# A two-layer decoder kernel: first squares moved from GpSimd to ScalarE, x loaded beside h, a written-out order for the first 24 product steps, gate products spread through hq1

## The reference, cut to what matters

```python
def trunk_layer(h, ...):
    xn = rms_norm(h, norm_pre_mix)          # h * rsqrt(mean(h*h) + eps) * w
    proj = xn @ w_in
    hq, hf, hi, hg, aq, ak, av, gq, gk, gv, g_lr, gr = jnp.split(proj, split_points, axis=-1)
    f = lb_h + (1.0 - lb_h) * jax.nn.sigmoid(heads(hf, HG_HEADS))
    ...
    log_a = jax.nn.log_sigmoid(g_lr @ gla_w_gate2 + gla_b_gate) / GLA_TAU
    o_g, s_gla_new = gated_linear_recurrence(gq * GLA_DK ** -0.5, gk, gv, log_a, s_gla)
```

## Time and profile before

| | |
|---|---|
| three runs | 1828.49, 1833.54, 1835.95 us; median 1833.54 us |
| the profiled execution's own time | 1833.51 us |
| its span (first to last instruction) | 1831.7 us |
| busy: PE, DVE, ACT, POOL | 1722.6, 845.8, 635.8, 100.8 us: 94%, 46%, 35%, 6% of the span |
| mean granted TensorE clock | 0.975 of full speed |

### The profile page before, as it was taken

The page is one execution under the profiler, slowest core; times in us unless marked ns, Lnnn a source line. Parts: engine busy times, 40 slices in busy tenths (PEclk is TensorE's granted clock), DMA queues, the critical chain, the costliest instruction groups (busy, mean ns, idle before and its releaser), DMA issues.

```text
span 1831.7 us, 35825 instructions
## 1 busy us (share of the span) xinstructions
PE 1722.6 (94%) x16090; PEld 1604.4 (88%) x16090; DVE 845.8 (46%) x1304; ACT 635.8 (35%) x934; POOL 100.8 (6%) x110
## 2 busy tenths in 40 slices
PE   5999888999999999999999998888999999999998
PEld 5888775588999999999988887755989999999988
DVE  5423776636423333335745147754354143333364
ACT  3323324645323222233443323255453231222332
POOL 3002301000000000000000131100000000000000
PEclk9999898999999999999999999989999999999999
DMA  6521509942745726362363124299319366355311
GB/s 252 188 63 57 185 2 364 377 181 70 280 156 196 240 82 221 103 205 81 113 222 104 62 69 156 90 377 345 122 63 349 100 221 222 115 185 183 122 64 64
DMA packets 61081, 304.55 MB, mean 166 GB/s; under 512 B 7169, under 2 KB 8833, under 8 KB 59265
## 3 DMA queue, kind: packets, MB, share of 16 engines
q1 hardware_dynamic: 53504, 201.80, 30.9%
q0 software_dynamic: 7424, 100.47, 16.0%
HBM read 291.62 MB, written 111.08 MB: 220 GB/s over the span
## 4 chain that ended last, share of the span: by engine, by line
PE 83%; DVE 9%; ACT 3%; issue 2%; DMA 2%; SPq 0%; POOL 0%; DVEq 0%; ACTq 0%
PE pair L1844 15%; PE pair L1846 15%; PE pair L1845 15%; PE pair L866 2%; PE pair L848 2%; PE pair L849 2%; PE pair L850 2%; PE pair L868 2%; PE pair L1155 2%; PE pair L870 2%; PE pair L1924 2%; PE pair L1023 2%; PE pair L794 1%; PE pair L1911 1%; PE pair L796 1%
## 5 line engine op out<-in xcount | busy, mean ns | idle before, releaser
L1844 PE MATMUL pair<-x_hi_part,w_hi_part 128*128 128x288 f32 x1088 | 322.2, 296 | 2.1 <-DVE tmp L2230 2.1
L1845 PE MATMUL pair<-x_lo_part,w_hi_part 128*128 128x288 f32 x1088 | 321.0, 295 | 0.0
L1846 PE MATMUL pair<-x_hi_part,w_lo_part 128*128 128x288 f32 x1088 | 319.9, 294 | 0.0
L2167 DVE TENSOR_TENSOR w_lo_part<-raw,w_hi_part 128x1024 fp32r<-128x1024 f32 x154 | 188.8, 1226 | 235.2 <-ACT w_hi_part L2011 235.1
L1844 PE MATMUL pair<-u_hi_part,w_hi_part 128*128 128x288 f32 x928 | 274.7, 296 | 0.0
L1845 PE MATMUL pair<-u_lo_part,w_hi_part 128*128 128x288 f32 x928 | 273.8, 295 | 0.0
L1846 PE MATMUL pair<-u_hi_part,w_lo_part 128*128 128x288 f32 x928 | 272.8, 294 | 0.0
L2011 ACT ACTIVATE w_hi_part<-raw 128x1024 fp32r<-128x1024 f32 x154 | 161.8, 1051 | 210.3 <-PE pair L1846 208.3
L1844 PEld LDWEIGHTS pair<-x_hi_part,w_hi_part 128*128 128x128 f32 x1088 | 203.8, 187 | 2.5 <-DVE tmp L2230 2.5
L1846 PEld LDWEIGHTS pair<-x_hi_part,w_lo_part 128*128 128x128 f32 x1088 | 204.9, 188 | 0.0
L1845 PEld LDWEIGHTS pair<-x_lo_part,w_hi_part 128*128 128x128 f32 x1088 | 204.3, 188 | 0.0
(11 more groups left out here) (295 smaller groups left out, 3440.9 us busy)
## 6 DMA issues: line engine op xcount, KB each, us to landing
raw<-w_units SPq DMA_DIRECT2D x210, 512.0 KB, 3.6
ck_out<-ck POOLq DMA_DIRECT2D x16, 3060.0 KB, 14.6
arena<-cv SPq DMA_DIRECT2D x24, 640.0 KB, 8.4
arena<-ck SPq DMA_DIRECT2D x18, 640.0 KB, 10.5
more<-ck SPq DMA_DIRECT2D x18, 640.0 KB, 13.4
tail<-cv SPq DMA_DIRECT2D x18, 640.0 KB, 9.6
h<-ck SPq DMA_DIRECT2D x12, 640.0 KB, 12.8
y_out<-h SPq DMA_DIRECT2D x16, 288.0 KB, 2.1
```

Source lines behind the costliest of these rows:

```text
L1844: nc.tensor.matmul(out, wh[:, cols], xh[:, k, t], start=n == 0, stop=False)
L1845: nc.tensor.matmul(out, wh[:, cols], xl[:, k, t], start=False, stop=False)
L1846: mm = nc.tensor.matmul(out, wl[:, cols], xh[:, k, t], start=False, stop=n == KT - 1)
L2167: return tt_(dst, src, hi.bitcast(F32), ALU.subtract).then_inc(*up(done, 1))
```

## The change

1. **Squares.** POOL's eight squares go. ACT squares (`square_first`): tiles 0 and 1 after it has done the leading parts of tiles 0 to 5; then unit 2, the leading parts of tiles 6 and 7, and the squares of tiles 2 to 7, then unit 3. DVE follows the same order and no longer waits for a square before a remainder.
2. **Loads.** x goes to a place of its own (X_FIRST, in the arena) instead of h; SP waits for par before it issues tiles 2-3; unit 2 goes ahead of tiles 6-7.
3. **Order of the first 24 steps.** `FIRST_STEPS` writes it out for each layer; `sum_pre` comes after 19 steps in layer 0 and after 12 in layer 1.
4. **Gate products.** The four matmuls of z0 and z1 go between the steps of hq1 (after its k = 1, 2, 3, 4) and into pairs 2 and 3.
5. **gq0's evac** and the split of unit 9 go between the second and the third scan.
6. **Units 0 and 1 of layer 1** are split behind gate5 and gate6 instead of gate6 and gate7.

Nothing in the diff adds or removes a product, and no warming product is in either kernel.

```diff
+FIRST_STEPS = [[(0, 0), (0, 1), (0, 2), (0, 3), (1, 0), (0, 4), (1, 1), (0, 5), (2, 0), (1, 2), (0, 6), (2, 1), (1, 3),
+                (2, 2), (1, 4), (2, 3), (1, 5), (2, 4), (1, 6), (2, 5), (0, 7), (1, 7), (2, 6), (2, 7)],
+               [(u, k) for u in range(2) for k in range(6)] + [(u, k) for u in range(2) for k in (6, 7)]
+               + [(2, k) for k in range(KT)]]
+SUM_AT = [19, 12]
-            return pair[3 if name == "sum_pre" else 2 if name in APART else Q[name] % 2]
+            return pair[3 if name in ("sum_pre", "z1") else 2 if name in APART or name == "z0" else Q[name] % 2]
...
+        X_FIRST = arena[:, 4608:4608 + KT * T].rearrange("p (k t) -> p k t", k=KT)
+        SQ_FIRST = tail[:, 5248:5248 + KT * T].rearrange("p (k t) -> p k t", k=KT)
...
             first_unit(0)
             pair_of_tiles(0)
+            sp.wait_ge(s_par0, 16)
             pair_of_tiles(1)
             first_unit(1)
             pair_of_tiles(2)
-            pair_of_tiles(3)
             first_unit(2)
+            pair_of_tiles(3)
...
-        @block.gpsimd
-        def _(pool):
-            for k in range(KT):
-                if k % 2 == 0:
-                    pool.wait_ge(s_x[k // 2], 16)
-                nc.gpsimd.tensor_tensor(SQ_FIRST[:, k], H[:, k], H[:, k], ALU.mult).then_inc(*up(sq_pre, 1))
+        def square_first(k):
+            nc.scalar.activation(SQ_FIRST[:, k], X_FIRST[:, k], ACT.Square).then_inc(*up(sq_pre, 1))
...
+            for k in range(6):                       # ACT, ahead of the layers
                 if k % 2 == 0:
                     act.wait_ge(s_x[k // 2], 16)
-                next_hi(act, k)
+                next_hi(act, k, X_FIRST)
                 if k == 3:
                     first_hi(act, 1, 0)
+            for k in range(2):
+                square_first(k)
...
-            for k in range(KT):                      # DVE, ahead of the layers
-                dve.wait_ge(sq_pre, k + 1)
-                next_lo(dve, k, 0)
+            for k in range(6):
+                next_lo(dve, k, 0, X_FIRST)
                 if k == 3:
                     first_lo(dve, 1, 0)
-                if k >= 1:
-                    add_square(dve, k, 0, lambda j: SQ_FIRST[:, j])
+            add_square(dve, 1, 0, lambda j: SQ_FIRST[:, j])
...
-                for s in range(KT + BEHIND[-1]):
-                    if s == KT - 2:
+                for n, (u, k) in enumerate(FIRST_STEPS[layer]):
+                    if n == SUM_AT[layer]:
                         sum_pre()
...
+                        if name == "hq1" and 1 <= k <= 4:
+                            z, half = divmod(k - 1, 2)
+                            mz = nc.tensor.matmul(home(f"z{z}")[:, half, 0:HALF], ...)
...
+                    act.wait_ge(s_x[3], 16)          # ACT, layer 0, between units 2 and 3
+                    next_hi(act, 6, X_FIRST)
+                    next_hi(act, 7, X_FIRST)
+                    for k in range(2, KT):
+                        square_first(k)
...
+                if layer == 0:                       # DVE, between units 2 and 3
+                    next_lo(dve, 6, 0, X_FIRST)
+                    next_lo(dve, 7, 0, X_FIRST)
+                    for k in range(2, KT):
+                        add_square(dve, k, 0, lambda j: SQ_FIRST[:, j])
...
                 for r in range(4):
+                    if r == 2:
+                        evac("gq0", 32.0 ** -0.5)
+                        split_w(9)
                     nc.vector.tensor_tensor_scan(B[:, r], RESET, LV[0][:, r], 0.0, ALU.mult, ALU.add).then_inc(*up(b_ready, 1))
-                evac("gq0", 32.0 ** -0.5)
-                split_w(9)
...
-                    if k >= KT - FIRST and layer + 1 < DEPTH:
-                        first_hi(act, k - KT + FIRST, layer + 1)
+                    if 5 <= k < 5 + FIRST and layer + 1 < DEPTH:
+                        first_hi(act, k - 5, layer + 1)
```

More of the change, by code:

```diff
@@ L797, in steps @@
                     return mm
-                for s in range(KT + BEHIND[-1]):
-                    if s == KT - 2:
+                begun = set()
+                for n, (u, k) in enumerate(FIRST_STEPS[layer]):
+                    if n == SUM_AT[layer]:
                         sum_pre()
[L802 to L807, removed]
+                    if u not in begun:
+                        begun.add(u)
+                        if layer > 0:
+                            pe.wait_ge(*at(lin_ev, u - 1))
+                        if u < FIRST:
                             pe.wait_ge(w0_split, FIRST * layer + u + 1)
-                        elif s == lag:
+                        else:
                             pe.wait_ge(*at(w_split, u - FIRST + 1))
-                        if 0 <= s - lag < KT:
-                            mm = steps(home(IN1[u]), w_hi_part(u), w_lo_part(u), s - lag)
-                            if s - lag == KT - 1:
-                                mm.then_inc(*up(lin_mm, 1))
+                    pe.wait_ge(xn_split, KT * layer + k + 1)
+                    mm = steps(home(IN1[u]), w_hi_part(u), w_lo_part(u), k)
+                    if k == KT - 1:
+                        mm.then_inc(*up(lin_mm, 1))
                 for i, name in enumerate(IN1):
@@ L823, in _ @@
                         mm = steps(ps, wh, wl, k)
-                    mm.then_inc(*up(lin_mm, 1))
-                    if name == "hq0":
-                        pe.wait_ge(*at(s_par0, 0))
-                        pe.wait_ge(*at(lin_ev, Q["gq1"] + 1))
-                        for z in range(2):
-                            ps = claim(f"z{z}")
-                            for half in range(2):
-                                mm = nc.tensor.matmul(ps[:, half, 0:HALF], par[64:80, W_G2 + P * z:W_G2 + P * (z + 1)],
-                                                      Q4[64:80, 3, half * HALF:(half + 1) * HALF], start=True, stop=True)
-                            mm.then_inc(*up(lin_mm, 1))
+                        if name == "hq1" and 1 <= k <= 4:
+                            z, half = divmod(k - 1, 2)
+                            mz = nc.tensor.matmul(home(f"z{z}")[:, half, 0:HALF], par[64:80, W_G2 + P * z:W_G2 + P * (z + 1)],
+                                                  Q4[64:80, 3, half * HALF:(half + 1) * HALF], start=True, stop=True)
+                            if half == 1:
+                                mz.then_inc(*up(lin_mm, 1))
+                    mm.then_inc(*up(lin_mm, 1))
                 for g in range(2):
```

58 lines of the change are left out of this document (30 added, 28 removed).

## The result

| | before | after |
|---|---|---|
| median of the runs made side by side | 1836.58 us (6 runs, 1828.49 to 1842.82) | 1819.42 us (6 runs, 1817.72 to 1821.93) |
| the profiled execution's own time | 1833.51 us | 1821.93 us |
| its span | 1831.7 us | 1820.1 us |
| busy PE, DVE, ACT, POOL | and the table above | 1724.5, 839.0, 640.0, 91.5 us |
| mean granted clock | 0.975 | 0.975 |

The changed kernel takes 0.9915 of the time of the one before (95% interval 0.9893 to 0.9937), 1819.42 us against a forecast of 1812.5 and a range that ended at 1819. More runs of the kernel before moved its median up: 1836.58, not the 1833.54 of the three runs shown.

The account below looks back on a forecast made before the run. TensorE, on 83% of the chain, was taken as the bound, with savings only where PE idles or runs at low clock. 9.5 + 0.85 + 2.2 + 5.2 + 0.85 + 2.4 = 21.0 off 1833.5 gave 1812.5 us, range 1807 to 1819.

Parts of the forecast that it names:

- part 3: gq0's evac, both layers: gk1 starts earlier, PE then stands 1.8 us ahead of vs0; saves 2.2 and 2.4 us.
- should shift as a whole: Everything after the changed places waits on semaphores, not times, so it moves earlier unchanged; forecast difference 0.
- part 2: z0 and z1 strewn in hq1, both layers: the clock holds, 10.15 us becomes 9.3; saves 0.85 each.
- part 1: Layer 0 up to the end of hq0: earlier PE start, no starving, new 1.75 us wait at hq0; saves 9.5 us.
- the table product: Rival, chance 0.18: POOL's product of the tables (L717) precedes DVE's remainder in layer 0, PE idles 4.7 us at hq0; 1817.
- the clock falls in more places: Rival, chance 0.08: half clock also at z and at the stalls of 1.75 and 1.8 us; all five places give 1820.
- Part 4: Start of layer 1: earlier splits and new order remove 3.6 us of idle and 1.6 of clock; saves 5.2 us.
- slower: Rival, chance 0.03: shifted short waits newly tip into half clock, 1.6 us each; with 24 of them 1851 us.

Follow-up runs that it names:

- a1: Changed kernel with only gq0's evac between the second and third scan, unit 9's split behind gk0's evac: 1813.93 us, 0.9871 of the kernel before.
- a3: Changed kernel with the squares back on POOL: 1828.19 us, 0.9950 of the kernel before.
- b1: Changed kernel with units 0 and 1 of layer 1 split late again, behind gate6 and gate7, new order kept: 1823.95 us in one run.
- b2: Changed kernel with layer 1's first 24 steps in the old order, early splits of units 0 and 1 kept: 1824.32 us in one run.
- a4: Changed kernel with the four gate matmuls in one block behind k = 1 of hq1, both layers: 1828.89 us in one run.
- c0: The changed kernel again, unedited: 1816.73 us, 0.9895 of the kernel before.
- b3: Changed kernel without SP's wait for par between the first two pairs of tiles of x: 1814.26 us in one run.
- d3: Changed kernel with POOL's cache copy released earlier, so its product of the tables gets in ahead of DVE: 1821.37 us in one run.
- b4: Changed kernel with a1's edit, layer 0's sum of squares after 14 steps instead of 19, and gate products in two pairs: 1812.17 us, 0.9869 of before.

## Why the forecast missed

Two terms failed that the sum put at nothing: the clock behind the new stall at vs0 (part 3), and everything behind vs0 ("should shift as a whole"). The gate products were mis-sized (part 2), and the base was 2.8 us too low. The waits that the change removes and makes were foreseen rightly, and a1, a3, b1 and b2 show their causes. That the parts add up to 20.2 for 21.0 is in part luck: 0.55 too much saved in part 1 stands against 1.1 too little in part 2.

**Part 1 (9.5, measured 10.05)** was right in its steps. PE started 0.7 us sooner than 9.6, the wait ahead of hq0 was 1.55 for 1.75, no step starved between. The slow matmuls at the start lasted 5.9 us for the 5.65 taken; over all eleven profiles of changed kernels it is 2.9 to 6.0 us, up to 1.5 us of time from one execution to the next. a3 shows the mechanism: the place of the squares is worth 6.65 us up to the sum, and in a3 the table product came ahead with it.

**Part 2 (0.85 in each layer, measured 0.28)** was right that the clock holds (a4), and wrong in the size. I had taken 0.53 for a product and 0.2 for a change of kind. A single one holds PE for 0.68 (42.77 to 43.45) and costs another 0.19 on both sides, 0.87 in all (9.87 less 6.4, over four), where 0.73 was reckoned. The price of 0.53 is that of a product in a row of its own kind. So the term of the gate products, 2.9 us a layer with the changes of kind, should have been 3.5.

**Part 3 (2.2 and 2.4, measured 2.08 and 2.32)** was right in the idle, 1.75 for 1.8, and in its cause (a1). The step that failed stands between the lines of it: a stall of 1.8 us ahead of vs0 was taken to leave the clock high, because one of 1.91 had the earlier trace rows. Both were followed by half clock in the first profile, 1.7 us each, one in layer 0, one in layer 1. In other profiles with the same idle the clock held in both layers (c0, b3, d3), fell in layer 1 alone (b1, b2, a3) or in both (a4): 7 of 16 places in all, 5 of 8 in layer 1. The idle of 1.56 at hq0 kept it in each of seven profiles. This is the rival *the clock falls in more places*, which had a chance of 0.08, for two of its five places. The ranking behind it (1.91 leaves the clock, 2.40 lowers it) was one row for each side, and the kernel before already contradicted it. PE stands 2.42 us ahead of 867.32 and the clock stays:

```profile
867.32 0.40 PE L1956 MATMUL pair<-x_hi_part,w_hi_extra 128*128 128x288 f32 x1 [2.42 <-DVE x_lo_part L2167]
```

```profile
862.00:885.00 23.00, 17.31 (x121) 16.04 (x121) 19.30 (x46) 9.51 (x19) 0.00 (x0) 1.00 0.19 65
```

In the same trace an idle of 1.89 us ahead of 304.54 (L1074) was followed by half clock from 306.5. The length of an idle alone does not tell.

**Part 4 (5.2)** was right to the tenth; b1 and b2 show that of its two causes the order counts for most, 4.8 us without the splits, against 1.6 for the splits without the order. (Before the wait PE did two full steps, not less than two, as 12 matmuls from 922.14 to 923.61 show; the sum does not use it.)

**"What follows should shift as a whole"** is the other step that failed. The same instructions, from vs0 to layer 1's start and from vs0 to the end, took 837.5 and 837.7 us in the one profile of before, and 839.3 and 841.9 on average in the eleven profiles with a changed front (835.8 to 848.1). c0 shows that this need not come with the edit: its two stretches took 837.07 and 838.29. In layer 1 the average is one of two groups, and what parts them is whether the clock fell at vs0 (the table under c0). So the two failed steps are not apart: the stall was worth more than its own stretch where the clock fell. In the 22 runs of before that have a clock listed, the time falls by about 1 us for each 0.001 of mean granted clock (1830.24 at 0.977, 1838.48 at 0.968). The rival *slower* had named the mechanism, stretches that newly tip, with the price of 1.6 each. I gave it only the case of 19 or more, and left the case of six out of the range. Six is what the first profile has: 92.2 us of half clock where the 88.7 of before, less the five stretches that went, leave 71.6. At 1.6 each that is 9.6, against the 8.6 measured.

**The base.** The sum was made against 1833.5 us, and the median over more runs of the kernel before is 1836.05 to 1836.58. By 1836.3, in place of 1833.5, the forecast would have been 2.8 higher, and with the parts as measured (20.2 for 21.0) 0.8 higher again: 1816.1. The two medians measured are 1819.42 and 1816.73. So of the 6.9 us by which the first is over the forecast, 3.6 are the base and the size of the parts, above all of z, and 3.3 are what is left for the stretches behind vs0 (0.6 by the second). How much of this is chance, and how much a lasting effect of where the stalls now fall, these runs leave open: two medians of one kernel 2.7 us apart, with ranges that overlap, do not tell it.

## What to carry to other kernels

When a piece of work is moved ahead of a stall, move that piece alone: a second one that rode along (the split of unit 9) waited for another engine and made a new stall of nearly 2 us, and undoing it was worth as much as the move. Follow each new stall through to the end before pricing it, and give a stall near 2 us half the price of a half-clock stretch on top (7 of 16 here), with a longer range towards slow: where the clock fell at vs0 of layer 1, the rest of the kernel was 7.8 us longer on average. Do not take one row as proof that an idle of that length is harmless. Matmuls of another kind are cheapest in pairs between full steps: single ones pay the change each time, four in a row cost the clock.

## What was not expected of the hardware

- One idle of 1.75 us was followed by half clock in one execution and by full clock in the next, in the same kernel; one of 1.48 with the sum's tiny products behind it was followed by it in b4, and one of 2.42 at 867.32 in the kernel before was not.
- The first matmuls ran at a pitch of 0.24 us for 2.9 to 6.0 us in kernels with the same start, while the clock column said 1.00.
- A VectorE operation on two elements a partition took 3.38 us beside a product of POOL (a3), and 2.62 us (d3), instead of 0.23 and 0.16.
- A single 16-row product takes PE 0.68 us, the second of a pair 0.48 (1.16 less 0.68).
